# Delta projection of a hybrid backbone step: convolution, logistic and product by token pieces, norm sums between the projections

## The reference

```python
y = conv(x, w)                    # 5 taps, centred, each channel by itself, zero padding
return jax.nn.silu(y)             # short_conv
...
qd, kd, vd = split_cols(qkv, (D_HEADS * D_DK, D_HEADS * D_DK, D_W))
qd = l2_norm(qd.reshape(B, T, D_HEADS, D_DK)) * (D_DK ** -0.5)
kd = l2_norm(kd.reshape(B, T, D_HEADS, D_DK))
```

## Time and profile before

| | us |
|---|---|
| median of 3 runs | 2261.18 |
| lowest and highest run | 2260.01, 2265.01 |
| the profiled execution | 2266.69 |
| its span, first to last instruction | 2264.9 |

### The profile page before, as it was taken

How to read it: one execution, slowest core, us unless ns; L and a number is a source line. 1 busy time by engine, 2 the same in 40 slices (tenths; PEclk the granted TensorE clock), 3 DMA queues, 4 the chain that set the end, 5 groups by cost and what they waited for, 6 DMA issues and landing times.

```text
span 2264.9 us, 30150 instructions
## 1 busy us (share of the span) xinstructions
PE 1988.2 (88%) x12212; PEld 1312.2 (58%) x12212; DVE 924.5 (41%) x1875; ACT 786.0 (35%) x1663; POOL 184.6 (8%) x259
## 2 busy tenths in 40 slices
PE   3978999997999989897979999878978977878898
PEld 1644555543565544774647765458567567476386
DVE  2665444312333364434643321462452462552442
ACT  2552444510222224313535551234333333432431
POOL 0000000000000000000000000025024033042000
PEclk8997999998999999998979999888988978988999
DMA  8020000021000224332020002210110100101232
GB/s 300 29 77 1 0 1 1 1 113 58 1 1 1 75 81 166 127 136 100 19 68 1 1 11 106 62 29 3 26 29 2 33 32 11 54 3 67 71 102 94
DMA packets 61292, 118.38 MB, mean 52 GB/s; under 512 B 5048, under 2 KB 27724, under 8 KB 61025
## 3 DMA queue, kind: packets, MB, share of 16 engines
q1 hardware_dynamic: 40033, 57.53, 7.7%
q0 software_dynamic: 8640, 33.75, 4.3%
q10 hardware_dynamic: 12480, 25.17, 3.1%
HBM read 96.47 MB, written 19.96 MB: 51 GB/s over the span
## 4 chain that ended last, share of the span: by engine, by line
PE 68%; issue 10%; DVE 5%; POOL 4%; PEld 4%; DMA 3%; ACT 3%; DVEq 1%; PEldq 1%; POOLq 0%; ACTq 0%; SPq 0%
PE ps L532 8%; PE ps L835 8%; PE ps L946 6%; PE ps L1003 6%; PEld ps L1761 4%; PE ps L1330 3%; PE ps L1170 3%; PE ps L1355 3%; PE ps L1171 3%; PE ps L1172 3%; PE ps L790 2%; PE ps L817 2%; PE ps L816 2%; PE ps L804 2%; DMA work<-in_w_mod 1%
## 5 line engine op out<-in xcount | busy, mean ns | idle before, releaser
L835 PE MATMUL ps<-work 128*128 128x512 f32 (+3 forms) x512 | 232.0, 536 | 0.0
L859 DVE TENSOR_REDUCE work<-ps 128x1 f32<-128x512 f32 (+2 forms) x272 | 145.2, 561 | 199.6 <-PE ps L790 198.9
L909 ACT ACTIVATE work<-ps 128x512 f32<-128x512 f32 (+3 forms) x256 | 132.1, 517 | 193.8 <-PE ps L817 141.7
L1761 PE MATMUL ps<-hT,wring 128*128 128x512 f32 (+1 forms) x576 | 190.1, 492 | 8.0 <-SPq L2134 5.5
L532 PE MATMUL ps<-wring,hT 128*128 128x512 f32 (+2 forms) x576 | 192.9, 493 | 0.0
L816 PE MATMUL ps<-qA,kA 128*128 128x512 f32 (+3 forms) x256 | 171.7, 671 | 2.1 <-ACT work L900 1.7
L1761 PEld LDWEIGHTS ps<-hT,wring 128*128 128x128 f32 x576 | 95.9, 193 | 103.6 <-issue 99.5
L532 PEld LDWEIGHTS ps<-wring,hT 128*128 128x128 f32 x576 | 109.1, 192 | 78.5 <-issue 70.3
L946 PE MATMUL ps<-hT,wring 128*128 128x512 f32 (+1 forms) x384 | 128.6, 497 | 4.0 <-DVEq L184 4.0
L1003 PE MATMUL ps<-wring,hT 128*128 128x512 f32 x288 | 125.8, 599 | 5.2 <-SPq L1549 3.4
L790 PE MATMUL ps<-kA,qA 128*128 128x128 f32 (+3 forms) x336 | 101.0, 351 | 27.0 <-DVE work L859 14.7
(11 more groups left out here) (291 smaller groups left out, 3499.6 us busy)
## 6 DMA issues: line engine op xcount, KB each, us to landing
work<-in_w_mod ACTq DMA_DIRECT2D x10, 2048.0 KB, 13.5
work<-in_x_sample SPq DMA_DIRECT2D x16, 512.0 KB, 6.5
wring<-in_w_in_even POOLq DMA_DIRECT2D x4, 2048.0 KB, 9.2
out_y_sample<-work SPq DMA_DIRECT2D x16, 512.0 KB, 3.0
work<-out_y_sample SPq DMA_DIRECT2D x16, 512.0 KB, 5.0
wring<-in_w_in_odd POOLq DMA_DIRECT2D x3, 2048.0 KB, 8.7
wring<-in_w_in_odd POOLq DMA_DIRECT2D x12, 512.0 KB, 6.4
yA_gated<-work SPq DMA_DIRECT2D x8, 576.0 KB, 3.3
```

The source lines that it names most:

```text
L835: pe.matmul(ps[:, 5 + c_, (qa - q0) * P:(qb - q0) * P], vaug[:, h // 4, kt, :], pT[i % 3][:, 0:(qb - qa) * P], start=(first and l == 0), s ...
L859: v.tensor_reduce(dst, src, AX.X, ALU.max).then_inc(sm("mx_used"), 1)
L909: act.activation(pT[i % 3][:, 0:n], ps[:, ST_BANKS[i % len(ST_BANKS)], 0:n], ACT.Exp, scale=0.125).then_inc(sm("p_done"), 1)
L1761: mm = pe.matmul(ps[:, PROJ_BANK[n], 0:m], w[:, k, b * P:(b + 1) * P], hT[:, k, o:o + m], start=(k == 0), stop=(k == KD - 1))
```

## The change

The change cuts the columns of a block in three segments, `SEGS` = 510, 514 and 130 columns: a segment is what can be convolved once the piece of the same number is projected, since a tap reaches two columns to either side. Convolution, logistic and product run by segment: nine of each instead of three. The unit norm becomes a function of its own that DVE calls between convolutions, the norm sums become a function that PE calls behind the projections n = 4 and n = 6, and they use other banks, since the former ones would still hold projections. The projection n = 8 goes to a bank that the norm sums of q have used, so it waits for the reciprocal norm of q. The order on ACT is written anew around the pieces.

```diff
--- before.py
+++ after.py
@@ -1743,7 +1743,9 @@
         NORM = [(a, min(512, NC2 - a)) for a in range(0, NC2, 512)]
 
         PROJ_BANK = (0, 1, 2, 3, 4, 5, 0, 1, 2)
-        SS_BANKS = ((3, 4, 5), (6, 7, 0))
+        SS_BANKS = ((6, 7, 2), (3, 4, 5))
+
+        SEGS = [(0, 510), (510, T_S), (T_S, NC2)]
         TURN_BANKS = ((6, 7, 5), (3, 4, 2))
         TURNS = [(0, 4), (4, 8), (8, 9)]
 
@@ -1752,27 +1754,32 @@
 
         def pre_pe(pe, h):
             w = weights(pe, f"dh{h}")
-            for n in range(9):
-                b, (o, m, _) = n // 3, TOK[n % 3]
-                if n >= 6:
-
-                    pe.wait_ge(sm("zp"), 9 * h + n - 5)
-                for k in range(KD):
-                    mm = pe.matmul(ps[:, PROJ_BANK[n], 0:m], w[:, k, b * P:(b + 1) * P], hT[:, k, o:o + m], start=(k == 0), stop=(k == KD - 1))
-                mm.then_inc(sm("zp_ps"), 1)
-            pe.drain().then_inc(sm("w_used"), 1)
-            for b in range(2):
-
-                pe.wait_ge(sm("zp"), 9 * h + (6, 7)[b])
+
+            def norms(b):
+                pe.wait_ge(sm("zp"), 9 * h + (3, 6)[b])
                 pe.wait_ge(sm("z_sq"), 2 * h + b + 1)
                 for n, (o, m) in enumerate(NORM):
                     mm = pe.matmul(ps[:, SS_BANKS[b][n], 0:m], ones, zblock(z_sq, b)[:, o:o + m], start=True, stop=True)
                 mm.then_inc(sm("z_ss"), 1)
+
+            for n in range(9):
+                b, (o, m, _) = n // 3, TOK[n % 3]
+                if n >= 6:
+
+                    pe.wait_ge(sm("zp"), 9 * h + n - 5)
+                if n == 8:
+                    pe.wait_ge(sm("z_rn"), 2 * h + 1)
+                for k in range(KD):
+                    mm = pe.matmul(ps[:, PROJ_BANK[n], 0:m], w[:, k, b * P:(b + 1) * P], hT[:, k, o:o + m], start=(k == 0), stop=(k == KD - 1))
+                mm.then_inc(sm("zp_ps"), 1)
+                if n in (4, 6):
+                    norms((4, 6).index(n))
+            pe.drain().then_inc(sm("w_used"), 1)
             for b in range(2):
                 if b == 0:
                     pe.wait_ge(sm("d_qkT"), h + 1)
                 else:
-                    pe.wait_ge(sm("z_silu"), 3 * h + 3)
+                    pe.wait_ge(sm("z_silu"), 9 * h + 9)
                     pe.wait_ge(sm("zp"), 9 * h + 9)
                 for n, (t0, t1) in enumerate(TURNS):
                     for t in range(t0, t1):
@@ -1788,20 +1795,22 @@
                 act.wait_ge(sm("zp_ps"), 9 * h + n + 1)
                 act.activation(zp[:, b, o:o + m], ps[:, PROJ_BANK[n], 0:m], ACT.Copy).then_inc(sm("zp"), 1)
 
-            def logistic(b):
-
-                act.wait_ge(sm("zc"), 3 * h + b + 1)
+            def logistic(b, x):
+
+                n = 9 * h + 3 * b + x
+                cols = slice(*SEGS[x])
+                act.wait_ge(sm("zc"), n + 1)
                 if b:
 
-                    act.wait_ge(sm("z_silu"), 3 * h + b)
-                act.activation(z_e, zblock(zc, b), ACT.Exp, scale=-1.0)
+                    act.wait_ge(sm("z_silu"), n - 2)
+                act.activation(z_e[:, cols], zblock(zc, b)[:, cols], ACT.Exp, scale=-1.0)
                 act.drain()
-                act.activation(z_e, z_e, ACT.Ln, bias=1.0)
+                act.activation(z_e[:, cols], z_e[:, cols], ACT.Ln, bias=1.0)
                 act.drain()
-                act.activation(z_e, z_e, ACT.Exp, scale=-1.0).then_inc(sm("z_sig"), 1)
+                act.activation(z_e[:, cols], z_e[:, cols], ACT.Exp, scale=-1.0).then_inc(sm("z_sig"), 1)
 
             def square(b):
-                act.wait_ge(sm("z_silu"), 3 * h + b + 1)
+                act.wait_ge(sm("z_silu"), 9 * h + 3 * b + 3)
                 act.activation(zblock(z_sq, b), zblock(zc, b), ACT.Square).then_inc(sm("z_sq"), 1)
 
             def rnorm(b):
@@ -1821,22 +1830,31 @@
                     mm = act.activation(d_Q[:, i, tiles, :], d_Q[:, i, tiles, :], ACT.Exp)
                 mm.then_inc(sm("s_E"), 1)
 
-            for n in range(3):
-                project(n)
-                decays(n)
+            project(0)
+            decays(0)
+            project(1)
+            decays(1)
+            logistic(0, 0)
+            project(2)
+            decays(2)
+            logistic(0, 1)
+            logistic(0, 2)
             project(3)
-            logistic(0)
+            square(0)
             project(4)
-            square(0)
-            for n in (5, 6):
-                project(n)
-            logistic(1)
+            logistic(1, 0)
+            project(5)
+            rnorm(0)
+            logistic(1, 1)
+            logistic(1, 2)
+            square(1)
+            project(6)
+            logistic(2, 0)
+            rnorm(1)
             project(7)
-            square(1)
+            logistic(2, 1)
             project(8)
-            rnorm(0)
-            rnorm(1)
-            logistic(2)
+            logistic(2, 2)
             for n, (t0, t1) in enumerate(TURNS):
                 act.wait_ge(sm("d_kv_ps"), 6 * h + n + 1)
                 act.activation(d_k[:, t0:t1, :], ps[:, TURN_BANKS[0][n], 0:(t1 - t0) * P].rearrange("p (t n) -> p t n", n=P), ACT.Copy)
@@ -1851,20 +1869,29 @@
                 v.memset(zp[:, :, a:a + 2], 0.0)
             v.drain()
 
-            def convolve(b):
-                v.wait_ge(sm("zp"), 9 * h + 3 * b + 3)
+            def convolve(b, x):
+                v.wait_ge(sm("zp"), 9 * h + 3 * b + x + 1)
+                lo, hi = SEGS[x]
                 for k in range(5):
                     tap = c_w[:, 12 * k + 4 * b + h:12 * k + 4 * b + h + 1]
                     if k == 0:
-                        mm = v.tensor_scalar(zcb[:, b, :], zp[:, b, k:k + NC2], tap, None, ALU.mult)
+                        mm = v.tensor_scalar(zcb[:, b, lo:hi], zp[:, b, k + lo:k + hi], tap, None, ALU.mult)
                     else:
                         v.drain()
-                        mm = v.scalar_tensor_tensor(zcb[:, b, :], zp[:, b, k:k + NC2], tap, zcb[:, b, :], ALU.mult, ALU.add)
+                        mm = v.scalar_tensor_tensor(zcb[:, b, lo:hi], zp[:, b, k + lo:k + hi], tap, zcb[:, b, lo:hi], ALU.mult, ALU.add)
                 mm.then_inc(sm("zc"), 1)
 
-            def silu(b):
-                v.wait_ge(sm("z_sig"), 3 * h + b + 1)
-                v.tensor_tensor(zblock(zc, b), zblock(zc, b), z_e, ALU.mult).then_inc(sm("z_silu"), 1)
+            def silu(b, x):
+                cols = slice(*SEGS[x])
+                v.wait_ge(sm("z_sig"), 9 * h + 3 * b + x + 1)
+                v.tensor_tensor(zblock(zc, b)[:, cols], zblock(zc, b)[:, cols], z_e[:, cols], ALU.mult).then_inc(sm("z_silu"), 1)
+
+            def unit_norm(dst, b, s):
+                v.wait_ge(sm("z_rn"), 2 * h + b + 1)
+                for o, n, x in ((0, T_S, 0), (T_S, T_P, 2)):
+                    a = b * NC2 + o + x
+                    mm = v.scalar_tensor_tensor(dst[:, o:o + n], z_rn[:, a:a + n], s, zc[:, a:a + n], ALU.mult, ALU.mult)
+                return mm
 
             v.wait_ge(sm("s_rows_in"), 16 * (h + 1))
             for g in range(NG):
@@ -1872,17 +1899,17 @@
                     t = NG * g + a
                     mm = v.scalar_tensor_tensor(d_A[:, i, t, :], d_Q[:, i, t, :], col(c_gc, i, t, h), cst("causal", i, P), ALU.subtract, ALU.min)
                 mm.then_inc(sm("s_D"), 1)
-            for b in range(2):
-                convolve(b)
-                silu(b)
-            convolve(2)
-            for dst, b, s in ((d_qT, 0, P ** -0.5), (d_kT, 1, 1.0)):
-                v.wait_ge(sm("z_rn"), 2 * h + b + 1)
-                for o, n, x in ((0, T_S, 0), (T_S, T_P, 2)):
-                    a = b * NC2 + o + x
-                    mm = v.scalar_tensor_tensor(dst[:, o:o + n], z_rn[:, a:a + n], s, zc[:, a:a + n], ALU.mult, ALU.mult)
-            mm.then_inc(sm("d_qkT"), 1)
-            silu(2)
+            for b in range(3):
+                convolve(b, 0)
+                if b == 2:
+                    unit_norm(d_kT, 1, 1.0).then_inc(sm("d_qkT"), 1)
+                convolve(b, 1)
+                silu(b, 0)
+                if b == 1:
+                    unit_norm(d_qT, 0, P ** -0.5)
+                convolve(b, 2)
+                silu(b, 1)
+                silu(b, 2)
             for n, (t0, t1) in enumerate(TURNS):
                 v.wait_ge(sm("d_kv_ps"), 6 * h + 3 + n + 1)
                 v.tensor_copy(d_v[:, t0:t1, :], ps[:, TURN_BANKS[1][n], 0:(t1 - t0) * P].rearrange("p (t n) -> p t n", n=P))
```

More of the change, by code:

```diff
@@ L1754, in pre_pe @@
             w = weights(pe, f"dh{h}")
+            def norms(b):
+                pe.wait_ge(sm("zp"), 9 * h + (3, 6)[b])
+                pe.wait_ge(sm("z_sq"), 2 * h + b + 1)
+                for n, (o, m) in enumerate(NORM):
+                    mm = pe.matmul(ps[:, SS_BANKS[b][n], 0:m], ones, zblock(z_sq, b)[:, o:o + m], start=True, stop=True)
+                mm.then_inc(sm("z_ss"), 1)
             for n in range(9):
@@ L1762, in pre_pe @@
                 mm.then_inc(sm("zp_ps"), 1)
```

(8 more changed lines are left out.)

## The result

| | before | after |
|---|---|---|
| median, same chip (4 runs each) | 2260.69 | 2278.68 |
| lowest and highest run | 2260.01, 2265.01 | 2278.12, 2282.55 |
| the profiled execution, its span | 2266.69, 2264.9 | 2278.12, 2276.3 |
| stage of heads 0 to 3, first projection to the next stage's first matmul | 64.06, 64.11, 62.63, 62.63 | 67.83, 67.99, 67.20, 67.84 |
| their sum | 253.43 | 270.86 |

All in us. The changed kernel takes 1.0079 of the time before (95% interval 1.0062 to 1.0097), 18.0 us more; the forecast was +17. The four stages are 17.4 us longer.

The account below looks back on a forecast made before the run. TensorE is busy for most of the span, so only its waits can be won; the ACT and DVE chain's +12.8 us and the clock's +4.4 make +17 on 2261.2, so 2278, range 2273 to 2283 (2264 to 2284 with rivals B to D).

Parts of the forecast that it names:

- The price of the pieces: On DVE, 0.218 us fixed per tap plus 1.042 ns a column; three convolution pieces take 9.58 us against 6.81 whole.
- C: Rival: short taps and passes on DVE and ACT cost half the fixed share, -18 us, so 2260; chance 0.08.
- D: Rival: more waiting between short dependent instructions on ACT and DVE, +13 us more, so 2291; chance 0.05.
- rival B: Same ACT and DVE chain, but TensorE's clock does not fall, so without the 4.4 us: 2274; chance 0.25.
- The chain: Delta stage, ACT and DVE alternating: +2.7 us each in heads 0 and 1, +3.7 in heads 2 and 3, 12.8 in all.
- The clock: TensorE's gap before the second norm sums halves its clock for about 3.3 us: 1.1 us a head, 4.4 in all.
- Rival A: Pieces hide the Delta stage's tail behind TensorE: stage 59.2 us, 4.9 less a head, 2241; chance 0.07.

Follow-up runs that it names:

- e6: Only block v in three pieces, q and k whole, norm sums behind all projections, calls reordered: 2251.50 us, 0.9959 of the kernel before.
- e8: The kernel before the change, unedited, profiled a second time: 2263.03 us, stage sum 251.99 us.
- e1: Changed kernel plus three matmuls with unread results in TensorE's gap before the second norm sums: 2274.71 us, 1.0057 of the kernel before.
- e2: Changed kernel with all nine pieces and TensorE's order kept, calls on ACT and DVE reordered: 2246.91 us, 0.9934 of the kernel before.
- e3: Only block v in pieces, norm sums behind n = 6 and n = 7, ACT and DVE calls reordered: 2247.19 us, 0.9936 of the kernel before.
- e4: Changed kernel with DVE's unit norm of q moved behind the last product of block k: 2262.01 us, 1.0002 of the kernel before.
- e7: e2 with `rnorm(0)` on ACT and the unit norm of q on DVE put back: 2265.48 us, 1.0019 of the kernel before.
- e10: Changed kernel with `rnorm(1)` moved ahead of logistic (2,0) on ACT: 2275.82 us, 1.0063 of the kernel before.
- e9: Changed kernel with the copy of projection n = 8 moved ahead of logistic (2,1) on ACT: 2274.81 us, 1.0056 of the kernel before.

## Why the prediction was right

**The price of the pieces.** Forecast 0.749 us for a tap of 510 columns (0.218 + 510 x 1.042 ns), measured 0.750; 0.353 for 130, measured 0.354. Four taps of 510 columns took 3.23 us (L1881 at 1645.08) against 4 x 0.749 + 3 x 0.075 = 3.22, so the waiting between them is as forecast. A logistic of 510 columns ran from 1620.67 to 1622.70 in head 1, 2.03 us against 2.00. The fixed cost is whole at 130 columns and the waiting no longer, so rivals C and D fall. (Their times, 2260 and 2291, lie outside the range of 2264 to 2284 that was to hold B to D; nothing rests on it.) The Trainium skill, "VectorE: DVE Perf Modes", section on the TRN2 errata, says that small tiles pay the fixed latency each and advises tiles of 512 elements or more; on the price the trace agrees (354 - 130 x 1.042 = 219 ns), but e6, with v in tiles of 510, 514 and 130 columns, is faster than whole blocks.

**The chain.** From the stage's start at 1600.27, head 1 has the copy of n = 5 at 34.77 (forecast 34.86), the copy of n = 6, right behind the square, at 43.64 (43.5), DVE's wait for `rnorm(1)` at 4.74 (nearly 5), TensorE's at 7.30 (about 7), and the next stage 1668.26 - 1665.23 = 3.03 us behind the last product (3.03). Head 0 came to 67.83 and head 1 to 67.99 against 66.8 + 1.1 = 67.9; heads 2 and 3 to 67.20 and 67.84 against 66.3 + 1.1 = 67.4. The sum is 17.4 against 17.2 (18.9 against the profile in e8, whose head 1 is shorter).

**The clock.** It fell behind all four gaps (norm sums of 3.87, 3.87, 3.65 and 3.87 us), as behind six of the seven gaps that the prediction counted in the trace of before (the earlier trace rows shows one of the six, and the seventh); rival B had 0.25 and failed. e1 shows the path that the forecast named, projection n = 7 late for convolution (2,1), and its size: 1.21 and 0.99 us in the two heads that can be compared, against 1.1.

**Rival A** needed the pieces to hide the tail: a stage of 59.2 us. The order on record does not do it, as the chain said; e2's order comes within 1.1 us of it in head 1, with 61.73, 60.33, 59.78 and 59.78 us in the four heads. The profile's half-idle engines were a real reserve, and what kept the change from it was where a few calls stand, not the pieces. The prediction named the waits and the price of each; it had not asked whether another order of the same calls would be free of them.

**What was off.** Head 3 started its projections at the low clock (31.0 us for the first five, against 29.5 in head 2), which the forecast had for heads 0 and 1 only. The profiled spans differ by 11.4 us, not 17, since the rest of the program was 6.0 shorter. e8 gave back only 2.3 of that, so it is not shown that the difference belongs to one execution. The forecast added the stages' 17 us to a median as if the rest kept its length; that the medians then differ by 18.0 is in part luck, and the stage sum, with the waits named in it, is the fairer test. The expectations for e2, e3, e4 and e6 lay 3 to 5 us above the medians, and that for e7 2.5 us below, although the stage sums came within 2.4 us of what was expected; the last section has the part of it that was found.

## What to carry to other kernels

Cutting a chain in pieces paid here only with every engine's queue ordered for it (e2 against the changed kernel): go through each queue and ask what stands behind an instruction that waits, and who waits for that. Put copies that free or feed another engine, and work that only the next step needs, so that neither stands between two links of the last chain. A wait that is removed is worth only what the next latest input leaves (e10: 2.8 us of idle time moved from one instruction to the next).

## What the runs showed of the hardware

The length of stages that no edit touched goes with the granted clock. From one Delta stage to the next lie 94.9 to 98.9 us, and which it is goes with the granted clock 72 to 80 us behind the stage's end. Of the 36 such stretches in twelve profiles, the 14 at the full clock went with 94.9 to 96.4 us, the 20 at 0.66 to 0.80 with 97.1 to 98.9, and two at 0.87 and 0.88 with 95.9. The stretch behind head 0 of the changed kernel, with 95.96 us to the next stage (busy PE; clock; DMA share, GB/s):

```profile
1576.32:1584.32 8.00, 7.77 (x63) 1.00 0.00 1
```

The same stretch of e9, with 98.52 us:

```profile
1571.44:1579.44 8.00, 7.02 (x44) 0.70 0.00 1
```

All three stretches of e9 are of this kind and none of the changed kernel's, so 295.33 - 288.46 = 6.9 of the 8.8 us that e9's stages gain are given back there (elsewhere it is 2.1 us shorter, which makes the 4.0 us by which its span is shorter). In e4 none is (287.47 us, against 291.35 and 292.85 in the two profiles of before), which goes with medians below the expected ones. This is read from the profiles; no run changed that clock by itself. The part ahead of the first Delta stage, with the same instructions in every kernel, took between 1431.4 us (e3) and 1439.3 (before); why stays open.

The first five projections take 31.0 us or 29.5, with a granted clock of 0.50 or 1.00 in their first 3 us. Head 0, behind an idle time of 2.48 us, has the longer time in all twelve profiles. Heads 1 to 3 come behind the same idle time of 1.83 to 1.84 us, and which of them has it differs: heads 1 and 3 in the changed kernel, none in e8. The Trainium skill, "TensorE: Matmul & The Clock Gate", Part 1 (the HAM clock gate), says that the number of matmuls at the low clock, counted at a kernel's start, differs between runs of one kernel; e8 against the first profile of before agrees in mid-kernel (head 1: 62.64 and 64.11 us).
